# Both expert tables streamed for latent chunks 1 and 2, gathered rows for chunks 3 and 4

## The reference

```python
def chunk(x):                                  # 128 tokens; 5 chunks: prompt (0), latents (1 to 4)
    q = (x @ w_q).reshape(PEER_CHUNK, PEER_HEADS, 2, PK_HALF)
    s = jnp.einsum('chpd,hpnd->chpn', q, sub_keys)          # 8 heads, 2 sides, 128 keys
    st, it = lax.top_k(s, PEER_TOPK)                        # 16 of 128 on each side
    cand = st[:, :, 0, :, None] + st[:, :, 1, None, :]      # 256 sums, again the best 16
    cidx = it[:, :, 0, :, None] * N_KEYS + it[:, :, 1, None, :]
    best, pos = lax.top_k(cand, PEER_TOPK)                  # (heads flattened as written)
    eidx = jnp.take_along_axis(cidx, pos, axis=-1)          # 128 experts for each token
    g = jax.nn.softmax(best, axis=-1)
    act = jax.nn.gelu(jnp.einsum('chkd,cd->chk', u_tab[eidx], x))
    return jnp.einsum('chk,chkd->cd', g * act, v_tab[eidx])
```

## Time and profile before

| | |
|---|---|
| median of 3 runs | 2459.42 us |
| profiled execution: span, first to last instruction | 2458.3 us |
| TensorE busy | 1778.0 us (72%) |
| VectorE busy | 1873.6 us (76%) |
| ScalarE busy | 514.3 us (21%) |
| POOL busy | 1037.4 us (42%) |
| moved by DMA | 753.43 MB, of it 536.94 MB by POOL's gathers |

### The profile page before, as it was taken

One profiled execution on the slowest core, in us unless ns is written; L12 is line 12 of the kernel. 1 busy time (PEld: TensorE's weight loads), 2 busy tenths in 40 slices (PEclk: granted clock), 3 DMA queues, 4 the chain that ended last, 5 costly groups with the idle time before them and its releaser, 6 DMA issues.

```text
span 2458.3 us, 20346 instructions
## 1 busy us (share of the span) xinstructions
PE 1778.0 (72%) x6013; PEld 1073.5 (44%) x6013; DVE 1873.6 (76%) x3933; ACT 514.3 (21%) x1283; POOL 1037.4 (42%) x1028
## 2 busy tenths in 40 slices
PE   7799889889887989891334666689999996000185
PEld 3578744444356438451012333556666664000032
DVE  2451588756789466889999999888687987999955
ACT  0563116440024000110004655710000000000111
POOL 0000000115534342443774776334344446777674
PEclk9899999899999999996566877899999998555599
DMA  9785772349955695866998999589999999999997
GB/s 279 250 274 193 233 231 87 113 135 319 353 182 180 215 330 177 288 250 211 384 410 285 390 411 404 200 300 411 414 411 414 411 411 411 410 408 406 364 404 304
DMA packets 296873, 753.43 MB, mean 306 GB/s; under 512 B 21502, under 2 KB 141102, under 8 KB 296244
## 3 DMA queue, kind: packets, MB, share of 16 engines
q0 software_dynamic: 147456, 536.94, 57.3%
q1 hardware_dynamic: 149308, 215.20, 25.0%
HBM read 740.72 MB, written 11.33 MB: 306 GB/s over the span
## 4 chain that ended last, share of the span: by engine, by line
DVE 37%; PE 29%; DMA 16%; POOL 8%; issue 6%; ACT 2%; DVEq 0%; SPq 0%; ACTq 0%; POOLq 0%
PE bank L788 12%; PE pair L788 6%; DVE big L1552 5%; DVE attn L1552 4%; DMA ring_more<-in_peer_u_dram,eidx 4%; DMA attn<-in_peer_u_dram,eidx 4%; DVE work L1552 3%; PE bank L971 3%; POOL work L2118 2%; DVE ring_more L1552 2%; POOL attn L2118 2%; PE bank L761 2%; POOL big L2118 2%; DMA attn<-in_peer_v_dram,eidx 2%; PE bank L1019 1%
## 5 line engine op out<-in xcount | busy, mean ns | idle before, releaser
L1019 PE MATMUL bank<-big,work 128*128 128x512 f32 x176 | 110.6, 767 | 369.4 <-ACT work L1091 266.3
L788 PE MATMUL pair<-big 128*128 128x128 f32 (+1 forms) x1280 | 361.8, 440 | 9.1 <-DVEq L1421 6.2
L2118 POOL DMA_INDIRECT h_all<-in_peer_u_dram,eidx x109 | 122.0, 1119 | 577.9 <-DVEq L1987 352.6
L788 PE MATMUL bank<-big 128*128 128x512 f32 (+1 forms) x1056 | 310.9, 453 | 34.4 <-DVEq L1421 22.7
L1064 PE MATMUL bank<-h_all,big 128*128 128x512 f32 x608 | 266.8, 595 | 4.6 <-DMA h_all<-in_peer_v_dram 4.6
L788 PEld LDWEIGHTS pair<-big 128*128 128x128 f32 x1280 | 197.3, 194 | 160.9 <-issue 158.6
L788 PEld LDWEIGHTS bank<-big 128*128 128x128 f32 x1056 | 169.2, 199 | 172.4 <-issue 165.0
L2118 POOL DMA_INDIRECT attn<-in_peer_u_dram,eidx x166 | 163.1, 983 | 165.5 <-DVE dots L1552 97.9
L1019 PEld LDWEIGHTS bank<-big,work 128*128 128x128 f32 x176 | 38.1, 235 | 427.0 <-issue 394.9
L1552 DVE CUSTOM_DVE_ANT_0 attn<-attn,pair 128x1024 f32<-128x1024 f32 x166 | 199.5, 1219 | 25.3 <-DMA attn<-in_peer_u_dram,eidx 23.0
L1064 PEld LDWEIGHTS bank<-h_all,big 128*128 128x128 f32 x608 | 180.5, 297 | 86.7 <-DMA h_all<-in_peer_v_dram 5.4
(11 more groups left out here) (311 smaller groups left out, 3172.7 us busy)
## 6 DMA issues: line engine op xcount, KB each, us to landing
big<-in_w_in_dram SPq DMA_DIRECT2D x44, 1024.0 KB, 6.5
h_all<-in_peer_v_dram SPq DMA_DIRECT2D x76, 512.0 KB, 6.8
big<-in_w_ada_dram SPq DMA_DIRECT2D x24, 1024.0 KB, 8.1
big<-in_peer_w_q_dram SPq DMA_DIRECT2D x16, 1024.0 KB, 5.6
gf_row<-in_peer_v_dram SPq DMA_DIRECT2D x26, 512.0 KB, 6.8
work<-in_peer_v_dram SPq DMA_DIRECT2D x26, 512.0 KB, 6.8
big<-in_w_rnn_o_dram SPq DMA_DIRECT2D x8, 1024.0 KB, 7.9
big<-in_w_attn_o_dram SPq DMA_DIRECT2D x8, 1024.0 KB, 6.4
```

The lines of the kernel that those rows point to most:

```text
L788: last = nc.tensor.matmul(u[:, 0:n], w[:, k, col:col + P], src[:, k, 0:n], start=(k == 0), stop=(k == KD - 1))
L1019: last = nc.tensor.matmul(psum[i][:, :], diag[:, (n - 1) % DIAGS, :], ring[r][:, i * 512:(i + 1) * 512], start=(k == first_by_tensor[c]), ...
L2118: g.indirect_dma_start(dst, None, ins["peer_" + table][0], bass.IndirectOffsetOnAxis(ap=eidx[:, c, k:k + 1], axis=0)).then_inc(landed, 16)
```

## The change

Chunks 1 and 2 no longer gather U. Both tables are streamed once, a tile of U and a tile of V for each of 128 steps n:

```diff
+            def turn_u(n):
+                pe.wait_ge(u_in[n % STREAM], 16 * (n // STREAM + 1))
+                if n:
+                    pe.wait_ge(uT_ready, 2 * n)
+                for k in range(KD):
+                    last = nc.tensor.transpose(uT_ps[:, k * P:(k + 1) * P], u_tile[n % STREAM][:, k * P:(k + 1) * P], ident[:, :])
...
+            def products(n):
+                pe.wait_ge(uT_ready, 2 * n + 2)
...
+                for k in range(KD):
+                    last = nc.tensor.matmul(a_ps[n % A_BUFS], uT[:, k, :], xT[:, k, :], start=(k == 0), stop=(k == KD - 1))
+            def sums(n):
+                pe.wait_ge(m_ready, n + 1)
+                pe.wait_ge(v_in[n % STREAM], 16 * (n // STREAM + 1))
...
+            for n in range(LAG, NKEY + LAG):
+                if n < NKEY:
+                    turn_u(n)
+                sums(n - LAG)
+                if n < NKEY:
+                    products(n)
```

```diff
+            PART_US, ROW_US = (1.8, 1.8, 1.8, 1.8, 4.3, 5.3, 2.8), 1.3
+            PACE = (2 * PAIRS * sum(PART_US) + ROW_US * (len(turns) - U3) + 40.0) / (NKEY - 4)
...
+            def spent(us):
+                clock[0] += us
+                while made[0] < NKEY and clock[0] >= PACE * (made[0] + 1):
+                    weigh(made[0])
+                    made[0] += 1
```

`PACE` comes to 6.955 us. The other parts:

```diff
-    RING = 29
+    RING = 12
-    SCALAR_HOTS = range(0, BUILDS, 2)
+    SCALAR_HOTS = range(2, BUILDS, 4)
-        by.append("tensor" if table == "v" and (c == 0 and k >= LEFT or c == C4 and k >= ALONE and k % 2 == 0) else "vector")
+        by.append("tensor" if table == "v" and c == 0 and k >= LEFT else "vector")
...
+        if turn < U3:
+            return range(6)
+        return [0, 1, 2, 4] + [6, 7, 8] * (turn >= BUILT) + [9, 10] * (turn >= C3_ROUTED) + [11] * (turn >= C4_ROUTED)
...
-            pe.wait_ge(sums_free, 2)
-            weighted_rows(len(turns))
...
-                V.tensor_tensor(hots[b % 2], both[:, :, m * BUILD:(m + 1) * BUILD].unsqueeze(3).to_broadcast(shape),
-                                iota128[:, :].unsqueeze(1).unsqueeze(1).to_broadcast(shape), ALU.is_equal).then_inc(hot_ready, 1)
+                V.tensor_tensor(hots[b % 2][:, 1, :, :], both[:, P + t0:P + t0 + BUILD].unsqueeze(2).to_broadcast([P, BUILD, P]),
+                                iota128[:, :].unsqueeze(1).to_broadcast([P, BUILD, P]), ALU.is_equal)
+                for t in range(BUILD):
+                    last = V.tensor_scalar(hots[b % 2][:, 0, t, :], iota128[:, :], both[:, t0 + t:t0 + t + 1],
+                                           weight[:, t0 + t:t0 + t + 1], ALU.is_equal, ALU.mult)
...
+                    if hp:
+                        search_second(hp - 1)
...
+            for pair in range(PAIRS):
+                settle(C1 + 1, pair, lambda i: hots_to(0, BUILDS * (3 * pair + i - 3) // (3 * PAIRS)))
```

More of the change, by code:

```diff
@@ L1729, in route, with search_second @@
                 between(6)
+            def route(c, pair, between):
+                for i in range(4):
+                    hp = 4 * pair + i
+                    topk(c - C1, hp, late34[:, c - C1 - 2, hp, :])
+                    between(i)
+                settle(c, pair, between)
+            def search_second(hp):
+                u = (1, "sc", hp)
+                dve.wait_ge(bank_free[bank[u]], use[u])
+                topk(1, hp, late2[:, hp, :])
             dve.wait_ge(x_in, 16)
@@ new lines, in spent, with ask, rows_beside @@
+            def spent(us):
[3 more added lines that the diff above has]
+                    made[0] += 1
+            def ask(what, c):
+                at = made[0] + 2
+                assert at >= LAG, (what, c)
+                asks.setdefault(min(at, NKEY), []).append((what, c))
+            def rows_beside(n):
+                for _ in range(n):
+                    rows(1)
+                    spent(ROW_US)
@@ new lines, in beside, with between, hots_to @@
+            def beside(n_rows):
+                def between(i):
+                    spent(PART_US[i])
+                    rows_beside(share(n_rows, i, PARTS))
+                return between
+            rows(U3 - next_turn[0])
+            routed(C1)
+            split_ids(C1)
+            next_hot = [0, 0]
+            def hots_to(i, end):
+                for m in range(next_hot[i], end):
+                    one_hots(i, m)
+                next_hot[i] = max(next_hot[i], end)
+            for pair in range(PAIRS):
+                settle(C1 + 1, pair, lambda i: hots_to(0, BUILDS * (3 * pair + i - 3) // (3 * PAIRS)))
@@ L2086, in _ @@
+            SPREAD = SLOTS // PAIRS
+            for pair in range(1, PAIRS):
+                route(C3, pair, beside(SPREAD))
             dve.wait_ge(final_in, 48)
             final(0, wk(4, 2))
-            step_end(C3)
-            for pair in range(1, PAIRS):
-                n_rows = share(SLOTS // 2, pair - 1, PAIRS - 1)
-                route(C4, pair, lambda i: rows(share(n_rows, i, PARTS)))
-            rows(SLOTS // 2)
+            routed(C3)
+            for pair in range(PAIRS):
+                route(C4, pair, beside(SPREAD // PAIRS))
@@ L2101, in _ @@
             final(C3, acc[1])
+            rows_beside(len(turns) - next_turn[0])
+            dve.wait_ge(row_used["vector"], count_after[sum_rows[C4][-1]])
+            add_sums(C4, acc4)
+            final(C4, acc4[1])
+            while made[0] < NKEY:
+                weigh(made[0])
+                made[0] += 1
             dve.wait_ge(sums_free, 2)
```

892 lines of the change are left out of this document (436 added, 456 removed).

## The result

The changed kernel takes 2586.35 us (median of 4 runs, 2584.34 to 2589.05) where the kernel before takes 2460.09 (2456.61 to 2463.17): a ratio of 1.051, 95% interval 1.0494 to 1.0526. 2587 was forecast. Its profiled execution has a span of 2586.0 us.

A forecast was written before the change was run, and what follows sets the result against it. Stream bounded by TensorE (981 us) and DMA (990) alike, DMA pacing rows: start 1433, chunk 3 to 1648, chunk 4 to 1783, rows to 2242 and 2476, weighs to 2566, ends 20, span 2586, median 2587 us; range 2470 to 2700.

The forecast's parts named there:

- First build, 1145: After score loop, topk and ids, the builds of the first chunk's W start at 1145 us.
- First chunk's builds, 200 us: 32 serial builds of W with 48 diagonal rows, 5.7 us each plus 16 at clock 0.85: 200 us, to 1345.
- Stream start, 1433: After the second chunk's builds, 88 us, the stream of tiles starts at 1433 us (1395 to 1545).
- chunk 3's 15 us: In chunk 3's three routed pairs, 15 us over for the first 32 rows, which have four slots; stage 215 us.
- A step of 7.80 us: TensorE's stream step: transposes 0.87, eight products of 0.437 and sums 3.43, together 7.80 us.
- Chunk 4's routing to 1783: Four pairs with 32 rows, 17.3 steps paced by TensorE: 135 us, to 1783, DMA only 258 GB/s.
- Rows at 9.37 us a step, to 2242: 256 rows alone, 47.9 DMA-paced steps of 9.37 us: 449, plus 10 for W's second half, to 2242.
- 13 weighs, 90 us: At the stream's end, chunk 4's end and 13 weighs take 90 us, to 2566, DMA idle by two thirds.
- The stream hides the rows: Rival: W ready before 1410 and row bytes spread over the whole stream, giving 2405 us; chance 0.12.
- TensorE bound throughout: Rival: TensorE paces the whole stream, W as late as reckoned, 2442 us, at worst 2554; chance 0.05.
- The clock falls: Rival: TensorE's idle gaps drop its mean clock to 0.8, a step 9.75 us everywhere, 2730 us; chance 0.15.
- The slots: Rival: gather slots bound the rows at 2.2 us each, a step 11.9 us, 2760 us; chance 0.08.

The follow-up runs named there:

- e1: Changed kernel with U tiles of which only 64 of 1024 columns are loaded; 2501.02 us, ratio 1.015 to the kernel before.
- e2: Changed kernel with four of the eight product matmuls of each step; 2554.9 us, ratio 1.0385 to the kernel before.
- e4: Changed kernel with the weighs paced at 5.52 us of VectorE's reckoning, so none are left for the end; 2536.69 us, ratio 1.0302 to the kernel before.
- v5: v4 with 4 instead of 8 one-hot builds on ScalarE, and U tiles 4 and 5 asked for before W's last store; 2456.8 us, ratio 0.9686.
- e6: Changed kernel with 7 ring slots open throughout, in place of 7, 9 and then 10; 2599.1 us, ratio 1.0243 to the kernel before.
- e7: Changed kernel with e4's pace and 16 rows a pair, in place of 8, beside chunk 4's routing; 2517.99 us, ratio 0.992 to the kernel before.
- v3: e7 with chunk 3's routing begun one pair earlier and 14 rows beside the second chunk's builds; 2502.6 us, ratio 0.9859 to the kernel before.
- v4: v3 with every second of the 48 prompt rows among the first chunk's builds done by VectorE there; 2476.01 us, ratio 1.0075 to the kernel before.
- e3: Changed kernel with 46 of 48 prompt rows moved from TensorE, among the first chunk's builds, to VectorE in the score loop; 2576.98 us, ratio 1.046.
- e5: Kernel before with 50 of the 52 chunk 4 V rows that TensorE took now on VectorE; 2526.61 us, ratio 0.9957; run again 2530.34 us, 0.9951.

## Why the prediction was right, point by point

- **First build, 1145**: ids turned at 1144.71. **First chunk's builds, 200 us**: the last build ended at 1340 for the forecast 1345. The clock came out 0.90, not 0.85. This term is right partly by luck: the prices named for it add to 5.4 and 9.0 us a build (1.5 x 2.93 + 1.05 and 1.5 x 4.73 + 1.9), not to 5.0 and 8.7.
- **Stream start, 1433**: TensorE's first turn in the stream was at 1444.76. The second chunk's builds ended on time; the fifth U tile was late by 10.57 us. The prediction had named that load behind the last store of W, but counted it within chunk 3's 15 us, and most of it was given back in that stage: weigh 27 is at 1652.00, where 26.4 steps were to end at 1648.
- **A step of 7.80 us**: 7.76 measured at the end, where TensorE is alone. The 275 ns that the prediction sets against its 0.11 us are no other price: one transpose lasts 272 to 273 ns in this trace too (L1062), and eight overlap, so that 0.11 us is their spacing. Weigh cost VectorE 0.60 us, not the 0.43 of the earlier trace rows; it hid under DMA's pace.
- **Chunk 4's routing to 1783**: weigh 44 at 1784.67, 17 steps of 7.80 from weigh 27. DMA moved 302 GB/s and not 258: half of what comes back of W, 4.2 MB, was sent for at 1706, here and not in chunk 3's stage, where the 82 MB had it.
- **Rows at 9.37 us a step, to 2242**: weigh 91 at 2238.72, so 47 steps of 9.66. One of them took 18.28, behind the other 4.2 MB of W, some 9 us over a step for the forecast's 10:

```profile
1988.28 0.91 SPq L724 DMA_DIRECT2D big<-w_later  x2
...
1991.69 0.60 DVE L1763 TENSOR_TENSOR attn<-work,big 128x256 f32<-128x256 f32 x1
...
2009.97 0.59 DVE L1763 TENSOR_TENSOR ktok<-work,big 128x256 f32<-128x256 f32 x1
```

The other 46 took 9.47 each, and the 23 steps from weigh 92 to 115, at 2466.95, 9.27. The forecast's step, DMA's bytes through 411 GB/s, is what e1 and e2 tell apart from TensorE: 85 us less against 31, and less than 3 of these in the rows. The prediction backed this ceiling with 404 to 414 GB/s "over 1000 us"; the longest such stretch of the earlier trace rows is ten slices, 615 us. The number held all the same.
- **13 weighs, 90 us**: weigh 115 stands at 2466.95, so 13 were left; weigh 116 to 128 took 2478.64 to 2559.64, and TensorE's last sums ended at 2568 for the forecast 2566. e4 removed them and got 50 us of the 90 back: DMA then needs the time elsewhere.
- **The rivals.** "The stream hides the rows" would have needed W by 1410; v5 has it there (1405), and its time is 2457, not the 2405 of the case: the two bounds of 981 and 990 us, both full at once, took 1022 from there to the last weigh, at 2427.56. "TensorE bound throughout" came in e4, as a second bound beside DMA, never alone. "The clock falls" did not come, at 0.95 and 0.93 in the two row stretches, though 0.93 is under the 0.95 that the prediction had named as a sign of being wrong: the steps there took 9.27 us, so it cost them nothing. In e2, with more idle time on TensorE, the clock was 0.86. "The slots" fell with e6.

The mechanism was right stage by stage, and the ends of the stages lie within 12 us of the forecast. That the sum comes within 1 us is luck: a late start of the stream and shorter row stretches cancel.

So the loss is one of order rather than of work: v5 does the same gathers, tiles and products and takes 2457 us. The kernel before, from the end of its scores to its V stage (windows as above):

```profile
1119.00:1171.00 52.00, 0.00 (x0) 0.00 (x0) 48.38 (x148) 1.45 (x6) 17.52 (x19) 0.53 0.52 179
1171.00:1395.00 224.00, 97.11 (x196) 42.47 (x196) 214.80 (x531) 57.13 (x163) 149.66 (x158) 0.64 0.95 367
1395.00:1617.00 222.00, 138.41 (x516) 85.33 (x516) 205.59 (x420) 138.60 (x431) 133.09 (x126) 0.80 0.88 335
```

That is 9 + 82 + 74, 166 MB in 498 us; the changed kernel moved 34 MB in the 288 us between 1145 and 1433, since the U rows of chunks 1 and 2 are gone and chunk 3's aren't routed yet. What remains, 407 MB from 1433 on, takes 990 us even if DMA never stops. e4, e7, v3, v4 and v5 took 50, 19, 15, 27 and 19 us out of it: e4 and e7 by another order within the stream, v3 by rows and routing moved before it, v4 and v5 by an earlier start (first weigh at 1461 us in v3, 1430 in v4, 1412 in v5). Steps between groups carry the chips' difference.

## What to carry to other kernels

Before replacing gathered rows by a stream, look at what those rows filled: bytes saved count only where DMA was full, and a stage that is a serial chain needs such rows beside it. A pace written into the order must leave nothing for the end, and is set from bytes of a step as well as from busy time. Work moved from one serial chain into another that also sets when a stage ends gains only the difference: 65 us less 55 in e3.

## What the hardware showed unexpectedly

An indirect DMA held POOL 0.93 to 1.03 us by group before the change, in rows of U beside the V stage, and 1.21 to 1.50 us in the row stretch after it (337.44 us for 256), with DMA equally full (404 and 408 GB/s). The largest groups of U rows:

```profile
L2118 POOL DMA_INDIRECT attn<-in_peer_u_dram,eidx x38 | 35.9, 944 | 38.7 <-DVE dots L1552 20.1 <-DVEq L1691 12.9 <-issue 5.7
```

```profile
L2189 POOL DMA_INDIRECT attn<-in_peer_u_dram,eidx x38 | 47.9, 1261 | 13.0 <-issue 10.7 <-DVE dots L1252 1.4 <-DVE big L1264 1.0
L2189 POOL DMA_INDIRECT big<-in_peer_u_dram,eidx x29 | 40.0, 1380 | 12.8 <-issue 6.7 <-DVE dots L1252 3.6 <-DVE big L1264 2.5
```

With about 0.3 us between them that is some 1.6 us a gather, close to the 1.8 us at which rows came (9.66 / 5.35): POOL was near to being a bound that the prediction never priced. In e2 it fell to 1.18 us (302.20 for 257) at the same 408 GB/s and no row came sooner, so it wasn't one. Why it differs is not shown.

The kernel before differs by 3.2% between chips, 2460 to 2465 and 2539 to 2541 us, while v5, on one where it takes 2541, was under both. Waits of 9.5 and 5.0 us at the same two VectorE instructions, ended by nothing within the core, stand in both traces taken on such chips of the kernel with e5's edit. ScalarE has them too: in e6, e7, v3 and v5, all profiled there, it stood 68, 87, 83 and 133 us before its moves of turned tiles with nothing in the core to end the wait, and in no trace taken where the kernel before takes 2460 to 2465. They cost the stream little: from 1420 to 2400 ScalarE's idle time before these moves is 761 us in v5 and 756 in v4, which has no such waits. What they are stays open.
